# A two-block transformer layer stack on one Trainium2 core: first modulation vectors in four column strips from eight load buffers, eighteen expert slots and an undivided gate bias

## What is computed

```python
x = first_block(x, c, ctx, c_ctx, ...)      # two layers
#   each layer: 6 modulation vectors = split(silu(c) @ ada_w[i] + ada_b[i]); the first layer also with c_ctx
#   layer 0: MLA attention over x and 256 ctx tokens, beside a gated short convolution; SwiGLU
#   layer 1: 2-D Fourier transform of four feature groups, then w_fourier; SwiGLU
return second_block(x, c_2, ...)            # one layer
#   sliding-window attention with sinks beside an RG-LRU, merged, w_out
#   mixture of experts: 32 experts, the 4 best per token
#     gu = x_e @ w_gu[e] + b_gu[e]; gate = min(gu[:, :1024], 7); up = clip(gu[:, 1024:], -7, 7)
#     y  = ((up + 1) * gate * sigmoid(1.702 * gate)) @ w_down[e] + b_down[e]
#   rms_norm(x, g_final)
```

## Time and profile before

| | |
|---|---|
| median of 3 runs | 1799.5 us (1798.65 to 1801.92) |
| the profiled execution | 1805.88 us, span 1804.0 us |
| TensorE busy | 92% of the span |
| VectorE, ScalarE, GpSimd busy | 42%, 24%, 7% |
| DMA | 586.59 MB, mean 325 GB/s; about 421 GB/s from 900 to 1780 us |
| expert loads | 384 of 1 MB |
| mean granted TensorE clock | 0.956 of full |

### The profile page before, as it was taken

One profiled execution on the slowest core, in us unless ns is written; L12 is line 12 of the kernel. 1 busy time (PEld: TensorE's weight loads), 2 busy tenths in 40 slices (PEclk: granted clock), 3 DMA queues, 4 the chain that ended last, 5 costly groups with the idle time before them and its releaser, 6 DMA issues.

```text
span 1804.0 us, 21857 instructions
## 1 busy us (share of the span) xinstructions
PE 1667.8 (92%) x8294; PEld 1003.7 (56%) x8294; DVE 760.4 (42%) x1190; ACT 430.2 (24%) x635; POOL 125.7 (7%) x155
## 2 busy tenths in 40 slices
PE   5999899999899999998999999999968898799876
PEld 2873588888778888876433433344423342344222
DVE  5666578777468776654211221222201120112022
ACT  3334544453344544343100000000000000000001
POOL 2842010000500000020000000000000000000000
PEclk8898999999999999998999999999988998899888
DMA  8723559885459887507999999999999999999995
GB/s 324 260 91 110 194 180 342 312 299 202 175 193 329 299 320 283 200 30 289 377 417 421 421 422 421 421 421 421 421 422 421 422 421 421 421 412 422 421 421 208
DMA packets 100429, 586.59 MB, mean 325 GB/s; under 512 B 12048, under 2 KB 13328, under 8 KB 44976
## 3 DMA queue, kind: packets, MB, share of 16 engines
q1 hardware_dynamic: 100336, 585.35, 82.1%
HBM read 584.26 MB, written 1.05 MB: 324 GB/s over the span
## 4 chain that ended last, share of the span: by engine, by line
PE 78%; DMA 10%; DVE 5%; SPq 3%; ACT 2%; issue 1%; DVEq 0%; ACTq 0%
PE psum L1245 23%; PE psum L1261 11%; PE psum L912 4%; PE psum L913 4%; PE psum L914 4%; SPq L423 3%; PE psum L1221 3%; DMA mraw<-gu_dram 3%; PE psum L1030 3%; PE psum L1274 3%; PE psum L933 2%; PE psum L935 2%; PE psum L934 2%; PE psum L730 2%; PE psum L732 2%; PE psum L731 2%
## 5 line engine op out<-in xcount | busy, mean ns | idle before, releaser
L1245 PE MATMUL psum<-mraw,xsat 128*64 128x512 f32 (+2 forms) x1640 | 415.2, 650 | 54.0 <-DMA mraw<-gu_dram 39.1
L1245 PEld LDWEIGHTS psum<-mraw,xsat 128*64 128x64 f32 (+2 forms) x1640 | 136.6, 144 | 307.8 <-issue 307.0
L1261 PE MATMUL psum<-mraw,xsat 128*64 128x512 f32 (+2 forms) x856 | 204.6, 619 | 16.8 <-DMA mraw<-dn_dram 9.6
L912 PE MATMUL psum<-wh,ah 128*128 128x512 f32 x352 | 139.7, 397 | 2.6 <-DVE al L1911 1.8
L1261 PEld LDWEIGHTS psum<-mraw,xsat 128*64 128x64 f32 (+2 forms) x856 | 68.1, 139 | 132.1 <-issue 130.1
L1800 POOL TENSOR_TENSOR wl<-raw,wh 128x256 fp32r<-128x256 f32 x136 | 114.5, 880 | 383.1 <-DVE work L1937 221.1
L913 PE MATMUL psum<-wl,ah 128*128 128x512 f32 x352 | 137.3, 390 | 0.0
L914 PE MATMUL psum<-wh,al 128*128 128x512 f32 x352 | 137.3, 390 | 0.0
L2454 DVE TENSOR_TENSOR oacc<-psum,oacc 128x512 f32<-128x512 f32 x60 | 38.6, 686 | 220.4 <-PE psum L1274 220.4
L1245 PE MATMUL psum<-mlast,xsat 128*64 128x512 f32 (+2 forms) x408 | 120.5, 646 | 0.0
L1967 DVE TENSOR_TENSOR wl<-raw,wh 128x1024 fp32r<-128x1024 f32 x88 | 103.6, 1219 | 33.5 <-ACT wh L1521 33.5
(11 more groups left out here) (368 smaller groups left out, 2437.2 us busy)
## 6 DMA issues: line engine op xcount, KB each, us to landing
mraw<-gu_dram SPq DMA_DIRECT2D x205, 1024.0 KB, 19.1
mraw<-dn_dram SPq DMA_DIRECT2D x107, 1024.0 KB, 25.5
araw<-ada_dram SPq DMA_DIRECT2D x128, 512.0 KB, 4.8
mlast<-gu_dram SPq DMA_DIRECT2D x51, 1024.0 KB, 19.7
raw<-ffa_dram SPq DMA_DIRECT2D x44, 1024.0 KB, 5.1
raw<-ffb_dram SPq DMA_DIRECT2D x44, 512.0 KB, 5.3
mlast<-dn_dram SPq DMA_DIRECT2D x21, 1024.0 KB, 23.3
raw<-blk_dram SPq DMA_DIRECT2D x34, 512.0 KB, 4.5
```

Source lines behind the costliest of these rows:

```text
L912: mm(o, ah3[:, j, tok], wh[:, w], start=(j == 0), stop=False)
L1245: last = mm(ps[4 + n][a * w:(a + 1) * w, :], xs[:, k * P + a * w:k * P + (a + 1) * w], slots[slot][:, i * 2 * D + n * 512:i * 2 * D + (n + ...
L1261: last = mm(ps[n][a * w:(a + 1) * w, :], at[:, k * P + a * w:k * P + (a + 1) * w], slots[slot][:, i * D + n * 512:i * D + (n + 1) * 512], ...
```

## The change

It has three parts.

1. **Rows of the first modulation.** All eight pairs have a buffer of their own. `ada_rows` puts the four products of a pair into four strips of 32 columns of one bank. The squares of x and ctx are added one after another on VectorE instead of reduced at once. Both rows are copied before block_hi(0). The convolution's first gate (four narrow blocks) moves ahead of kv, so blocks 3 to 6 are narrow and 7 to 9 wide. The ctx norm's scale and shift go to ScalarE (`ctx_hi`), between block_hi(3) and block_hi(7), its low parts to VectorE between the evacuations of blocks 0 to 3, and VectorE's ada operations from blocks 0 to 7 to blocks 4 to 11. VectorE makes the low part of block 0. The sums of squares of q and ckv move with their blocks. (They also feed `cqs`: the squares of ckv are now behind block_hi(13) on ScalarE.)
2. **The gate/up bias** is held undivided, as `[128, 512]` with one quarter of the columns per 32 partitions; its four products take 32 rows each, in four row strips. Lines 1717 and 2351 go.
3. **Eighteen slots.** One more whole slot is among those loaded early. The last one is made of two pieces of 1024 columns in `work` and in the norm's root tiles, loaded by two issues. `rout` moves into `at`, and `act_c` is `gate_c`.

The core of the diff:

```diff
-B_Q, B_KV, B_KPE, B_CB, B_CC, B_CU = 0, 3, 5, 6, 10, 14
+B_Q, B_CB, B_KV, B_KPE, B_CC, B_CU = 0, 3, 7, 9, 10, 14
...
-NFIRST = 5
+NFIRST = 8
...
-NSLOT, NWIDE = 16, 13
-EARLY_SLOTS, NEXT_SLOTS = (0, 1, 2, 12, 5, 13, 14, 15), (8,)
+NSLOT, NWIDE, NLAST = 18, 13, 4
+SPLIT_SLOT = NSLOT - 1
+EARLY_SLOTS, NEXT_SLOTS = (0, 1, 2, 12, 5, 13, 14, 15, 16), (8,)
...
+        act_c = gate_c
+        split_slot = [wflat[:, 3 * D:4 * D], roots[:, :, :].rearrange("p a t -> p (a t)")]
+        rout = at[:, 512:768].rearrange("p (j e) -> p j e", j=DJ)
...
             def ada_pair(k):
-                if k >= NFIRST:
-                    sp.wait_ge(s_adp, k - NFIRST + 1)
...
                 wait(sp, m["chunk"], before)
-                sp.dma_start(slots[slot], src).then_inc(s_slot[slot], 16)
+                if slot == SPLIT_SLOT:
+                    if before == 0:
+                        sp.wait_ge(s_ht, 4)
+                    for half in range(2):
+                        sp.dma_start(split_slot[half], src[:, half * D:(half + 1) * D]).then_inc(s_slot[slot], 16)
+                else:
+                    sp.dma_start(slots[slot], src).then_inc(s_slot[slot], 16)
...
-            sp.dma_start(bgr[0:NEXP, :], bgu_d).then_inc(s_par, 16)
-            sp.dma_start(bgr[NEXP:2 * NEXP, :], bgu_d).then_inc(s_par, 16)
+            sp.dma_start(bgu[:, :], bgu_d).then_inc(s_par, 16)
...
-            sp.wait_ge(s_bgh, 1)
+            sp.wait_ge(s_par, EXP_IN)
...
+            def ada_rows(k):
+                g, j = k // 4, 2 * (k % 4)
+                pe.wait_ge(s_afirst[k], 16)
+                for a in range(2):
                     for half in range(2):
+                        strip = 64 * a + 32 * half
+                        last = mm(ps[4 + g][strip:strip + 32, :], cpad[:, j + a, :],
+                                  afirst[k][:, a, half * 512:(half + 1) * 512], start=(j == 0), stop=(j == 6),
+                                  skip_group_check=True)
+                last.then_inc(s_adp, 1)
...
-            ada_rows(0)
+            for k in range(2):
+                ada_rows(k)
             pe.wait_ge(s_con, 16)
-            pe.wait_ge(s_sqx, 1)
-            mm(ps[3][:, :], ones, kpe[:, :], start=True, stop=True).then_inc(s_sum, 1)
+            pe.wait_ge(s_sqx, 7)
+            mm(ps[3][:, :], ones, work[:, 0, :], start=True, stop=True).then_inc(s_sum, 1)
+            for k in range(2, 6):
+                ada_rows(k)
             row_columns(0)
-            ada_rows(1)
+            for k in range(6, 8):
+                ada_rows(k)
             row_columns(1)
...
+            for b in range(B_O):
+                block_product(b, 2 * T if B_KV <= b <= B_KPE else T, fresh={0: (s_hl, 0), B_KV: (s_hlx, 0)}.get(b))
+                if b == B_KV:
+                    for j in range(3):
+                        pe.wait_ge(s_cqs, j + 1)
+                        last = mm(ps[3][:, 0:T], ones, sqf[:, j * T:(j + 1) * T], start=(j == 0), stop=(j == 2))
+                    last.then_inc(s_cqsum, 1)
+                if b == B_CC:
+                    for j in range(2):
+                        pe.wait_ge(s_cqs, 4 + j)
+                        last = mm(ps[4][:, :], ones, pbuf[:, j, :], start=(j == 0), stop=(j == 1))
+                    last.then_inc(s_cqsum, 1)
...
                     for n in range(4):
-                        mm(ps[4 + n][:, :], sel[:, u % 2, :], bgu[:, n * 512:(n + 1) * 512], start=True, stop=False,
+                        rows = slice(32 * n, 32 * n + 32)
+                        mm(ps[4 + n][:, :], sel[rows, u % 2, :], bgu[rows, :], start=True, stop=False,
                            skip_group_check=True)
...
             ada_row(0)
+            ada_row(1)
             for b in range(3):
                 block_hi(b)
-            ada_row(1)
             h_hi(0)
...
+            def ctx_hi(j):
+                act.wait_ge(s_ntx, j + 1)
+                link(A(work[:, j, T:2 * T], work[:, j, T:2 * T], ACT.Identity, bias=modx[:, j:j + 1], scale=gsx[:, j:j + 1]))
+                A(ah3[:, j, T:2 * T], work[:, j, T:2 * T], ACT.Copy).then_inc(s_hhx, 1)
+
+            for b in range(3, 7):
                 block_hi(b)
...
+                ctx_hi(2 * (b - 3))
+                ctx_hi(2 * (b - 3) + 1)
+            block_hi(7)
+            for j in range(3):
                 act.wait_ge(s_ev, j + 1)
...
+                A(sqf[:, j * T:(j + 1) * T], cq[:, j, :], ACT.Square).then_inc(s_cqs, 1)
+            for b in range(8, 11):
                 block_hi(b)
             act.wait_ge(s_cqsum, 1)
             A(rt[:, 0:T], ps[3][:, 0:T], ACT.Sqrt, bias=V("eps"), scale=1.0 / QR).then_inc(s_cqrt, 1)
+            for b in range(11, 14):
+                block_hi(b)
+            for j in range(2):
+                act.wait_ge(s_ev, B_KV + j + 1)
+                A(pbuf[:, j, :], ckv[:, j, :], ACT.Square).then_inc(s_cqs, 1)
+            block_hi(14)
...
-            act.wait_ge(s_par, EXP_IN)
-            A(bgu[:, :], bgr[:, :], ACT.Copy).then_inc(s_bgh, 1)
...
-            for b in range(B_F):
+            pool.wait_ge(s_lo, 1)
+            for b in range(1, B_F):
                 block_lo(b)
...
-                            mod_ready(0)
-                            mod_ready(1)
+                            dve.wait_ge(s_hi, 1)
+                            TTn(wl[:, 0:D], raw[:, 0:D], f32(wh[:, 0:D]), ALU.subtract).then_inc(s_lo, 1)
+                            first_mods()
...
-            dve.wait_ge(s_sq, DJ)
-            V_.reduce_sum(kpe[:, :], work[:, :, :].rearrange("p j t -> p t j"), AX).then_inc(s_sqx, 1)
+            for j in range(1, DJ):
+                dve.wait_ge(s_sq, j + 1)
+                wait(dve, s_sqx, j - 1)
+                TTn(work[:, 0, :], work[:, 0, :], work[:, j, :], ALU.add).then_inc(s_sqx, 1)
             norm(0, _V["n1"], 0, hl=0)
-            ctx_norm()
...
-                if b < 8:
-                    ada(ADA_FIRST + b)
+                if b < 4:
+                    ctx_lo(2 * b)
+                    ctx_lo(2 * b + 1)
+                elif b < 12:
+                    ada(ADA_FIRST + b - 4)
...
-                if j == 3:
-                    dve.wait_ge(s_bgh, 1)
-                    TTn(bgu[NEXP:2 * NEXP, :], bgr[NEXP:2 * NEXP, :], f32(bgu[NEXP:2 * NEXP, :]), ALU.subtract
-                        ).then_inc(s_bgl, 1)
```

More of the change, by code:

```diff
@@ L109, in schedule @@
                 free[i] = p * n + done[st]
-                where[p, st, a] = (i, 16 * count[i])
+                where[p, st, a] = (i, (32 if i == SPLIT_SLOT else 16) * count[i])
     return done, loads, where, n
@@ L128 @@
 _n = 0
-for _name, _m in [("ident", 128), ("ones", 128), ("triu", 128), ("iota", 128), ("iota32", 32), ("ekey", NEXP), ("capkey", NEXP), ("capval", NEXP), ("erow", 1), ("first", 2), ("pick", 2)]:
+for _name, _m in [("ident", 128), ("ones", 128), ("triu", 128), ("iota", 128), ("iota32", 32), ("ekey", NEXP), ("capkey", NEXP), ("capval", NEXP), ("erow", 1), ("first", 2), ("pick", 4)]:
     _C[_name] = _n
@@ L292, in build, with slot_columns @@
         wflat = work[:, :, :].rearrange("p j t -> p (j t)")
-        gate_c, up_c, sig_c, act_c = [wflat[:, i * D:(i + 1) * D] for i in range(4)]
-        slots = [mraw[:, i, :] for i in range(NWIDE)] + [mlast[:, i, :] for i in range(NSLOT - NWIDE)]
+        gate_c, up_c, sig_c = [wflat[:, i * D:(i + 1) * D] for i in range(3)]
+        act_c = gate_c
+        slots = [mraw[:, i, :] for i in range(NWIDE)] + [mlast[:, i, :] for i in range(NLAST)]
+        split_slot = [wflat[:, 3 * D:4 * D], roots[:, :, :].rearrange("p a t -> p (a t)")]
+        rout = at[:, 512:768].rearrange("p (j e) -> p j e", j=DJ)
+        def slot_columns(slot, c0):
+            if slot == SPLIT_SLOT:
+                return split_slot[c0 // D][:, c0 % D:c0 % D + 512]
+            return slots[slot][:, c0:c0 + 512]
         bdn = ymo[0:NEXP, :]
@@ L1245, in up_product @@
                             last = mm(ps[4 + n][a * w:(a + 1) * w, :], xs[:, k * P + a * w:k * P + (a + 1) * w],
-                                      slots[slot][:, i * 2 * D + n * 512:i * 2 * D + (n + 1) * 512], start=False,
+                                      slot_columns(slot, i * 2 * D + n * 512), start=False,
                                       stop=(k == 7), skip_group_check=True)
@@ L1261, in down_product @@
                                 last = mm(ps[n][a * w:(a + 1) * w, :], at[:, k * P + a * w:k * P + (a + 1) * w],
-                                          slots[slot][:, i * D + n * 512:i * D + (n + 1) * 512], start=(k == 0),
+                                          slot_columns(slot, i * D + n * 512), start=(k == 0),
                                           stop=(k == 7), skip_group_check=True)
@@ L1447, in _ @@
             A(rt[:, :], ps[4][:, :], ACT.Sqrt, bias=V("eps"), scale=1.0 / KVR).then_inc(s_cqrt, 1)
-            for b in range(13, B_O):
+            for b in range(15, B_O):
                 block_hi(b)
@@ L1518, in ffn_hi @@
```

(6 more changed lines are left out.)

152 lines of the change are left out of this document (53 added, 99 removed).

## The result

| | before | after |
|---|---|---|
| median, lowest to highest | 1804.7 us (1798.65 to 1808.92) | 1793.35 us (1789.6 to 1797.81) |
| ratio, 95% interval | | 0.9945 (0.9928 to 0.9961) |
| profiled execution, span | 1805.88 us, 1804.0 us | 1793.97 us, 1792.2 us |
| mean granted TensorE clock | 0.956 | 0.961 |

The change makes the kernel faster by 9.9 us, with an interval from 7 to 13. The forecast was 8.7. Measured side by side with the new kernel, the old one has a median of 1804.7 instead of the 1799.5 that the forecast started from, so the comparison is by the ratio and not by the distance to 1799.5. (The two medians of the table are 11.3 us apart, which is inside the interval too.) Executions of one kernel lie up to 10 us apart. The two profiled ones are 11.8 us apart in span, and the part on the clock says where the difference from 9.9 can come from.

The account below looks back on a forecast made before the run. TensorE and its feeders were taken to bound the kernel up to about 850 us, then the DMA stream of expert weights. Front 0.7 + bias 3.0 + slots 5.0 = 8.7 us, from 1799.5 to 1790.8 us, range 1781 to 1800.

Parts of the forecast that it names:

- Part 1: First modulation's rows: pairs cost about 1 us warm, 1.8 cold; VectorE's next stage at 37.5, about 6 us gained.
- Part 2: Norm(0) to block 7: GpSimd slows VectorE, norm(0) done at 46.5, block 7 starts at 64; gain 9.4 us without a stop.
- Part 3: Behind block 10: TensorE waits 6 us for ckv squares behind block 13's load; 8.5 us given back, front nets 0.7.
- Rival (a): Front: ckv squares don't wait for block 13 or the ada load comes sooner; all 9.4 us kept, 1782.3 us; chance 0.17.
- Part 4: Loop ahead of the experts: without the bias split 3.0 us gained; bias products in row strips take 1 to 1.3 us.
- Part 5: Expert loads: eighteen slots put the stream two loads ahead, 2 x 2.49 = 5.0 us gained at its end.
- standstill cut to about half: Sign at the first DMA standstill, at 843 us: two early loads would cut it to about half.
- Rival (c): Expert bias products: row strips run one after the other, +3.7 us in sum, 1803.2 us; chance 0.12.
- Rival (b): Expert loads: slots give nothing, as SyncE gets the order late or unit 0's loads are delayed; 1795.8 us; chance 0.16.

Follow-up runs that it names:

- e5: Changed kernel with ScalarE's squares of ckv ahead of block_hi(12) and, in SyncE's queue, block loads 8 to 13 ahead of the ada loads: 0.9889 of the old kernel's time.
- e2: Changed kernel with ScalarE's two squares of ckv moved ahead of block_hi(12): 0.9935 of the old kernel's time.
- e3: Changed kernel with the four gate/up bias products over all 128 rows, so one after another (bias values wrong): 1.003 of the old kernel's time.
- e4: Old kernel with the split of its bias table moved behind the squares and norm of x: 0.9996 of the old kernel's time.
- e1: Changed kernel with sixteen slots again, all else as changed: 0.9971 of the old kernel's time.
- e6: Changed kernel with seventeen slots, the one in two pieces left out: 0.9947 of the old kernel's time.
- e7: Changed kernel with five dummy TensorE products after the first merge sum to keep the clock up: 0.9947 of the old kernel's time.
- e8: Changed kernel with the edits of e5 and e7 together: 0.9883 of the old kernel's time.

## Why the prediction was right, point by point

**Part 1, the rows.** Forecast: 1 us a pair warm and 1.8 cold, VectorE's next stage at 37.5. Measured: 1.03, 1.93 and 37.66. The last pair was at hand at 30.5, as worked out from one pair per 2.55 us.

**Part 2, the chain behind it.** Forecast: norm(0) done at 46.5, block 2 at 54, block 7 from 64. Measured: 45.07 (43.98 + 1.09), 52.55, and 64.28. The operations that ran beside GpSimd took 0.7 to 0.9 us and the others 0.41. The guess was that seven fall beside it; it was five. The 1.5 us by which block 2 came sooner aren't lost behind it: TensorE ran four blocks of 2.88 us and waited only 0.25 us, for GpSimd, ahead of block 7. It is the forecast's own 54 and 64 that don't fit each other, since 54 plus four such blocks is 65.5.

**Part 3, the wait that took the place.** Forecast: about 6 us behind block 10, block 17 at 116, and the chain by which it comes about. Measured: 5.88 us and 115.60, and the chain is that of the rows above. Forecast too: without the stop, 107.3; e5 has 108.01. So the mechanism was right; that 116 was hit within 0.4 us has some luck in it, since block 7 started on time only by the two slips of part 2. What the forecast had not seen is that undoing only the last link would not do. It put all 8.5 us to the wait of the squares; e2 shows 2.6 us for them and e5 another 5.0 for the order of the loads. Rival (a) made the same step: it gave the squares not waiting for block 13 the whole 8.5 us, and e2, in which they don't wait for it, keeps 2.6 of them.

**Part 4, the bias.** Forecast 3.0 us for the loop, measured 3.03. Its parts were 0.7 us of idleness (0.60) and a sum of 1 us (0.59 + 0.70). It is on the path, as said: from norm 4 to the first slot it is 23.58 us before and 23.57 after. Within that, the choice of experts takes 2.3 us longer, since TensorE ran at the lower level from 829 to 842 us, and the first products take 2.3 us less, since it ran at the full one from 842 on. The bias product was put at 1 to 1.3 us by the column strips and measured at 1.29 and 1.14. The row of e3 gives 3.60 / 1.14 = 3.2 times for the four strips. The Trainium skill, "TensorE: Matmul & The Clock Gate", Part 3, has 3.07 times for four tiles of 32 rows, and the trace agrees. Of the drain that the Trainium skill, "TensorEngine Tiling (Array Packing)", Key Properties, names for a change of tiling mode the trace shows nothing: the products before, in and behind the strips follow each other at 841.61 and 842.83 without a gap, though with ends that the profile models. e4, with the old bias, takes 1.19 us for its second bias product (at 884.01) where the strips take 1.14, so the new form costs no more than the old.

**Part 5, the slots.** Forecast 5.0 us, measured 4.7 (medians) and 3.64 (traces). The step that was off is the equal worth of both slots: 3.15 and 0.49. The two loads went out as said, and the second standstill stayed. The sign "standstill cut to about half" came true, 11.0 us to 5.7, but it proves little: e1 without the slots has 6.2. The forecast's 9.5 us of standstill was that of before; with the loop 3.0 us shorter, less was left for the two loads to fill.

**The sum.** 8.7 forecast, 9.9 measured (7 to 13). By the traces the change's own terms are 1.2 us from the front at block 17 (0.5 to 1.0 in e1, e3, e6 and e7, which have the same front; 0.7 had been forecast), 3.0 for the loop and 3.6 for the slots, so 7.8, and at most 9.4 with the 1.6 of the last point below. The forecast's 8.7 is near the measured time partly by luck: the slots were put 1.4 us too high, the front 0.5 too low, and what else the measured time holds was in none of its terms. Of the other 3.7 of the 11.6 us at the last product, 2.8 are differences in the clock, of both signs, and 0.9 are spread over stages where I saw no single cause:

- From norm 1 to norm 2 it is 61.55 us before and 58.94 after. TensorE stops for 2.8 us in both. In before it comes back at the lower level, in after at the full one. Windows of before, then of after, at that stop:

```profile
495.00:500.00 5.00, 3.50 (x16) 3.53 (x17) 2.33 (x5) 1.33 (x4) 3.11 (x4) 0.56 0.19 43
500.00:505.00 5.00, 5.00 (x35) 5.00 (x34) 2.99 (x4) 0.42 (x1) 0.00 (x0) 0.75 0.69 271
```

```profile
493.30:498.30 5.00, 3.47 (x29) 3.50 (x30) 2.65 (x6) 1.35 (x4) 3.14 (x4) 1.00 0.17 39
```

  The stage takes 58.9 to 59.0 us in e2, e5 and e8, 59.6 in e3 and e7, and 60.2 to 60.4 in e1, e4 and e6. Since e3, e6 and e7 have the front of after and e4 the old kernel, the 2.6 us can't be put down to the change.
- At the first merge it goes the other way, 1.4 us: 15.14 before and 16.5 after, 13.56 where the clock holds.
- At the second standstill it gives 1.6 us. From the first slot to the load that ends the standstill it is 897.70 - 852.93 = 44.77 us in before and 890.16 - 847.04 = 43.12 in e1, which also has sixteen slots. Before has a stretch at the lower level there, e1 has none; windows of each, and of e4:

```profile
892.00:895.00 3.00, 3.00 (x8) 0.89 (x9) 0.58 (x3) 0.00 (x0) 0.00 (x0) 0.50 0.85 352
```

```profile
889.00:892.00 3.00, 3.00 (x18) 1.00 (x16) 0.00 (x0) 0.00 (x0) 0.00 (x0) 1.00 0.31 52
```

```profile
886.00:889.00 3.00, 3.00 (x10) 0.80 (x8) 0.00 (x0) 0.00 (x0) 0.00 (x0) 0.50 0.62 249
```

  From that load to the last product before and e1 both take 885.7 us. e4 has the lower level there too, and 44.86 us. So both kernels with the old bias have this stretch and none of the eight with the new one does. It may belong to the change; why wasn't looked into, and one execution of each can't prove it.

A median evens this out only in part, and with the interval of 3 us either way the terms can't be had from medians. They can be had from segments of the traces between two markers, where the clock of each is known.

**Rival (c), row strips in turn.** It was held unlikely and didn't come, but e3 tried its mechanism: 13.5 us by the trace where 12.4 had been worked out. The size is right and its parts are not: bias 0 costs 2.4 us and not 5.9 (it ran at the full clock), the second standstill 3.3 and not 4, and the later stream, put at 2.5, has nearly all the rest. The queue of loads took in less than was worked out from its 11.3 us to landing.

**Rival (b), slots give nothing,** fell with e1.

Open: what the slot in two pieces costs, why VectorE's operation took 6.49 us in e2, what decides in which executions TensorE's clock falls at a stop of 2.8 us, and whether the clock at the second standstill comes with the new bias.

## What to carry to other kernels

A load that stands in one queue behind another one waits for the other's releaser as well. When a consumer moves later, look at every load that stands behind its buffers in the queue, and test the queue's order and not only the last wait that the profile names. Where a stream is bound by DMA, look for its standstills before adding buffers: here the first extra buffer took most of what the standstill gave (3.15 us of 3.64). And when two parts of a change touch the same standstill, run each alone before reading its length as the work of one. Where the question is some 3 us and executions scatter by 10, compare segments between markers in traces, with the clock of each beside them.

## What the runs showed of the hardware

- A stop of TensorE of 2.8 to 3.0 us at the same instruction was followed by the lower clock level in some of the ten profiled executions and not in others. Where it was, the stage took 0.6 to 2.9 us longer (59.6 to 61.55 us against 58.9 between norms 1 and 2, 15.14 and 16.5 against 13.56 at the merge).
- Four float32 products of 32 rows and 512 columns in four row strips take 1.14 us at the full clock, four over 128 rows 3.60 us.
- A VectorE operation that takes 1.18 us in after lasted 6.49 us in e2, to the end of a train of twenty GpSimd pieces, far beyond the doubling seen in the earlier trace rows. Why isn't known.
